# Where the small matrix products of a side chain stand among the wide ones on TensorE (hybrid attention layer, one core)

## What is computed

```python
h = rms_norm(x, pre_w); proj = h @ w_in           # 1024 -> 6152 columns
# branch 1: stick-breaking attention, 8 heads of 64, blocks of 128 keys
z = q @ k.T * 64**-0.5
suffix = cumsum(log_keep, reverse=True) - log_keep # log_keep = -softplus(z), causal
o_sb = (exp(log_sigmoid(z) + suffix) @ v) * silu(gate)
# branch 2: gated delta rule, 4 heads of 128, chunks
q, k, v = silu(causal_conv4(...)); q, k l2-normalised
m = strict(beta * (k @ k.T) * decay)               # unit lower triangular system
u, w = solve(m, [v * beta, k * beta * exp(g)])
for c in chunks:                                   # state S
    v_new = u[c] - w[c] @ S
    o[c]  = (q[c] * exp(g)) @ S + intra[c] @ v_new
    S     = S * exp(g_last) + (k[c] * exp(g_last - g)).T @ v_new
o_gd = rms_norm(o) * silu(gate)
merged = sigmoid(m1) * (o_sb @ w_sb) + sigmoid(m2) * (o_gd @ w_gd)
x = x + rms_norm(merged @ w_out)
```

## Time and profile before

| What | Value |
|---|---|
| median of three runs | 1246.81 us (1245.89 to 1248.23) |
| the profiled execution | 1248.23 us, span 1246.9 us |
| PE busy | 1188.6 us, 95% |
| DVE, ACT, POOL busy | 518.8, 557.8, 471.6 us |
| share of PE in the chain that ended last | 84% |
| wide products L411 | 1536 |

### The profile page before, as it was taken

One profiled execution on the slowest core, in us unless ns is written; L12 is line 12 of the kernel. 1 busy time (PEld: TensorE's weight loads), 2 busy tenths in 40 slices (PEclk: granted clock), 3 DMA queues, 4 the chain that ended last, 5 costly groups with the idle time before them and its releaser, 6 DMA issues.

```text
span 1246.9 us, 15061 instructions
## 1 busy us (share of the span) xinstructions
PE 1188.6 (95%) x5783; PEld 931.0 (75%) x5783; DVE 518.8 (42%) x1092; ACT 557.8 (45%) x1012; POOL 471.6 (38%) x291
## 2 busy tenths in 40 slices
PE   6999999999989999989999999989899999999997
PEld 6777767767657788878677777657888888888886
DVE  4057376575564314153233333332621111644444
ACT  5356466375477653243344444343432222433332
POOL 3344344234343344552222221222444444644441
PEclk9999999999999999989999999978899999999999
DMA  8221120211121233622111111111233333423211
GB/s 240 77 68 52 35 80 23 68 52 34 51 68 35 68 102 102 219 68 56 51 52 51 52 51 51 52 51 51 68 102 93 93 101 101 127 93 102 95 58 68
DMA packets 139801, 95.35 MB, mean 76 GB/s; under 512 B 8801, under 2 KB 124874, under 8 KB 139730
## 3 DMA queue, kind: packets, MB, share of 16 engines
q1 hardware_dynamic: 136112, 89.18, 24.5%
q10 hardware_dynamic: 3618, 5.22, 1.3%
HBM read 91.49 MB, written 2.88 MB: 76 GB/s over the span
## 4 chain that ended last, share of the span: by engine, by line
PE 84%; DVE 8%; ACT 4%; POOL 1%; issue 1%; DMA 0%; ACTq 0%; DVEq 0%
PE bank L411 24%; PE bank L1166 12%; PE bank L1148 12%; PE bank L440 5%; PE bank L808 4%; PE bank L817 3%; PE bank L833 2%; DVE g L1865 2%; PE bank L946 2%; PE bank L631 2%; PE bank L1179 1%; PE bank L958 1%; PE bank L622 1%; DVE g L1862 1%; PE bank L447 1%
## 5 line engine op out<-in xcount | busy, mean ns | idle before, releaser
L2388 POOL TENSOR_TENSOR ring<-raw_ring,ring 128x1024 fp32r<-128x1024 f32 x159 | 386.3, 2433 | 607.0 <-ACT ring L1192 607.0
L411 PE MATMUL bank<-hT,ring 128*128 128x512 f32 x1536 | 406.4, 410 | 4.1 <-POOL ring L2388 3.4
L411 PEld LDWEIGHTS bank<-hT,ring 128*128 128x128 f32 x1536 | 282.7, 192 | 75.0 <-issue 16.4
L1192 ACT CAST ring<-raw_ring 128x1024 fp32r<-128x1024 f32 x160 | 166.7, 1044 | 116.2 <-PE bank L1166 93.8
L1166 PE MATMUL bank<-ring,ring_u 128*128 128x512 f32 x672 | 154.0, 391 | 0.0
L1148 PE MATMUL bank<-hT,ring 128*128 128x512 f32 x672 | 152.5, 389 | 0.0
L1166 PEld LDWEIGHTS bank<-ring,ring_u 128*128 128x128 f32 x672 | 126.2, 188 | 27.6
L1148 PEld LDWEIGHTS bank<-hT,ring 128*128 128x128 f32 x672 | 126.1, 188 | 26.1
L2365 DVE TENSOR_TENSOR ring_u<-u,ring_u 128x1024 fp32r<-128x1024 f32 x32 | 82.4, 2582 | 76.0 <-ACT ring_u L1744 76.0
L2370 DVE TENSOR_TENSOR u<-u 128x512 f32<-128x512 f32 x32 | 22.9, 715 | 139.2 <-ACT u L1751 139.2
L440 PE MATMUL bank<-hT,ring 128*128 128x256 f32 x576 | 70.4, 284 | 2.3 <-DVE hT L1790 2.3
(11 more groups left out here) (297 smaller groups left out, 1615.2 us busy)
## 6 DMA issues: line engine op xcount, KB each, us to landing
raw_ring<-in_w_in SPq DMA_DIRECT2D x144, 256.0 KB, 3.3
raw_ring<-in_w_up SPq DMA_DIRECT2D x64, 256.0 KB, 3.3
raw_ring<-in_w_down SPq DMA_DIRECT2D x64, 256.0 KB, 2.8
raw_ring<-in_w_out SPq DMA_DIRECT2D x32, 256.0 KB, 2.8
x<-in_x SPq DMA_DIRECT2D x4, 512.0 KB, 5.7
raw_ring<-in_w_branch_sb SPq DMA_DIRECT2D x8, 256.0 KB, 2.9
raw_ring<-in_w_branch_gdn SPq DMA_DIRECT2D x8, 256.0 KB, 3.3
x<-in_x ACTq DMA_DIRECT2D x4, 512.0 KB, 6.0
```

The costliest lines, as they stand in the source:

```text
L411: p = pe.matmul(bank, m.slab_k8(n % 4)[:, a, k, :], m.hT[:, b, k, :], start=term == 0, stop=term == 23)
L1192: act.copy(m.ring[:, q, 0, :], m.raw_ring[:, q, :]).then_inc(s.slab_hi[q], 1)
L2388: pool.tensor_tensor(m.ring[:, q, 1, :], m.raw_ring[:, q, :], m.ring[:, q, 0, :].bitcast(F32), ALU.subtract).then_inc(s.slab_lo[q], 1)
```

## The change

Only numbers in `tiles.to` change, and a few calls of it are added or taken out, in the three loop passes and in the merge stage. No instruction is added or removed; DVE, ACT, POOL and the DMA queue keep their lists word for word. On PE the same products stand in another mixture.

```diff
     for i in range(3):
         tiles = Tall(SLABS_A + 8 * (i + 1), 8, tile_a_free(8 * (i + 1)))
-        tiles.to(14)
+        tiles.to(6)
         delta_decay(i)
-        tiles.to(27)
+        tiles.to(16)
         delta_decay_rows(i)
...
-        tiles.to(78)
+        tiles.to(83)
         delta_gram(i)
-        tiles.to(88)
         stick_z(i, 0, 2)
...
-        tiles.to(126)
+        tiles.to(119)
         delta_level_first(i, 4)
+        tiles.to(122)
         stick_log(i, 0, 1)
...
-        tiles.to(140)
+        tiles.to(130)
         stick_log(i, 0, 0)
...
-        tiles.to(146)
+        tiles.to(137)
         delta_solve(i)
-        tiles.to(150)
+        tiles.to(139)
         delta_chunk(i, 0)
+        tiles.to(142)
         delta_from_state(i, 1)
+        tiles.to(144)
         delta_chunk(i, 1)
...
-        tiles.to(165)
+        tiles.to(160)
         delta_o_sum(i)
         tiles.rest()
...
-    tiles.to(64)
+    tiles.to(74)
     delta_k_sum(i)
     delta_v_rows(i)
-    tiles.to(91)
+    tiles.to(94)
     delta_gram(i)
...
-    tiles.to(148)
     delta_level_first(i, 5)
-    tiles.to(164)
+    tiles.to(150)
     stick_log(i, 0, 1)
     stick_log(i, 1, 1)
     delta_level_second(i, 5)
```

More of the change, by code:

```diff
@@ L651, in tensor_program @@
         stick_v_rows(i)
-        tiles.to(60)
+        tiles.to(68)
         stick_z(i, 0, 3)
@@ L656, in tensor_program @@
         delta_v_rows(i)
-        tiles.to(76)
+        tiles.to(81)
         stick_log(i, 0, 3)
         stick_log(i, 1, 3)
-        tiles.to(78)
+        tiles.to(83)
         delta_gram(i)
-        tiles.to(88)
         stick_z(i, 0, 2)
@@ L666, in tensor_program @@
         stick_av(i, 1, 3)
-        tiles.to(102)
+        tiles.to(106)
         stick_log(i, 0, 2)
         stick_log(i, 1, 2)
-        tiles.to(105)
+        tiles.to(112)
         stick_z(i, 0, 1)
@@ L683, in tensor_program @@
         stick_av(i, 1, 1)
-        tiles.to(128)
+        tiles.to(126)
         delta_level_first(i, 5)
-        tiles.to(140)
+        tiles.to(130)
         stick_log(i, 0, 0)
@@ L692, in tensor_program @@
         delta_level_first(i, 6)
-        tiles.to(143)
+        tiles.to(133)
         delta_level_second(i, 6)
-        tiles.to(146)
+        tiles.to(137)
         delta_solve(i)
-        tiles.to(150)
+        tiles.to(139)
         delta_chunk(i, 0)
+        tiles.to(142)
         delta_from_state(i, 1)
+        tiles.to(144)
         delta_chunk(i, 1)
+        tiles.to(147)
+        delta_from_state(i, 2)
+        tiles.to(149)
+        delta_chunk(i, 2)
         tiles.to(152)
-        delta_from_state(i, 2)
+        delta_from_state(i, 3)
         tiles.to(154)
-        delta_chunk(i, 2)
-        tiles.to(157)
-        delta_from_state(i, 3)
-        tiles.to(159)
         delta_chunk(i, 3)
-        tiles.to(165)
+        tiles.to(160)
         delta_o_sum(i)
@@ L722, in tensor_program @@
     delta_decay(i)
-    tiles.to(18)
+    tiles.to(20)
     delta_decay_rows(i)
-    tiles.to(20)
     stick_v_rows(i)
-    tiles.to(56)
+    tiles.to(54)
     delta_q_sum(i)
-    tiles.to(64)
+    tiles.to(74)
     delta_k_sum(i)
     delta_v_rows(i)
-    tiles.to(91)
+    tiles.to(94)
     delta_gram(i)
-    tiles.to(103)
+    tiles.to(106)
     stick_z(i, 0, 3)
     stick_z(i, 1, 3)
-    tiles.to(113)
+    tiles.to(120)
     stick_log(i, 0, 3)
     stick_log(i, 1, 3)
-    tiles.to(114)
+    tiles.to(126)
     stick_z(i, 0, 2)
     stick_z(i, 1, 2)
-    tiles.to(118)
     stick_av(i, 0, 3)
@@ L747, in tensor_program @@
     delta_level_first(i, 4)
+    tiles.to(138)
     stick_log(i, 0, 2)
@@ L750, in tensor_program @@
     delta_level_second(i, 4)
-    tiles.to(137)
+    tiles.to(143)
     stick_z(i, 0, 1)
@@ L761, in tensor_program @@
     delta_level_second(i, 5)
+    tiles.to(155)
     stick_z(i, 0, 0)
@@ L765, in tensor_program @@
     stick_av(i, 1, 1)
-    tiles.to(166)
     delta_level_first(i, 6)
-    tiles.to(176)
+    tiles.to(169)
     stick_log(i, 0, 0)
@@ L771, in tensor_program @@
     delta_level_second(i, 6)
+    tiles.to(175)
     stick_av(i, 0, 0)
     stick_av(i, 1, 0)
-    tiles.to(184)
     delta_solve(i)
-    tiles.to(195)
+    tiles.to(187)
     delta_chunk(i, 0)
-    tiles.to(198)
+    tiles.to(193)
     delta_from_state(i, 1)
-    tiles.to(202)
+    tiles.to(199)
     delta_chunk(i, 1)
-    tiles.to(207)
+    tiles.to(205)
     delta_from_state(i, 2)
-    tiles.to(216)
+    tiles.to(211)
     delta_chunk(i, 2)
-    tiles.to(220)
+    tiles.to(215)
     delta_from_state(i, 3)
@@ L789, in tensor_program @@
     delta_chunk(i, 3)
-    tiles.to(232)
+    tiles.to(230)
     delta_o_sum(i)
```

## The result

| Kernel | Median | Runs |
|---|---|---|
| before | 1247.52 us (1245.89 to 1248.24) | 4 |
| changed | 1259.16 us (1258.36 to 1260.37) | 4 |

The ratio is 1.0104, interval 1.0087 to 1.0121. The forecast was 1254.4 us, within 1249.5 to 1260. So the time is 4.8 us above the one named, and the change is 11.6 us, where 7.6 were forecast. The sign was right, and most of the waits came where they were expected. The likeliest case had a range of its own, 1252 to 1257 us, and that missed. The wide range held narrowly: over all 37 executions of the changed kernel on record the median is 1260.0 us (1257.87 to 1267.25), 12.5 us above the kernel before. Run again beside the kernel before on another chip, the changed one was also 12.5 us slower by the medians, ratio 1.0096 (1.0081 to 1.0111).

A forecast was written before the change was run, and what follows sets the result against it. PE was taken to bound the kernel, so only its waits, clock and returns to wide products could change the time. Passes +4.35, merge stage +3.2 and clock 0 made +7.55 us: 1254.4 us for the median, range 1249.5 to 1260.

The forecast's parts named there:

- The likeliest case: Whole kernel: the forecast itself, a median of 1254.4 us from the summed terms, given 42%.
- end of a pass, L600 to L517: Each pass's end: five more wide products fall into waits and are missing elsewhere, -1.15 us a pass.
- Gram products to level 4, with the port: Each pass: twelve fewer covering products give 1.9 us of new waiting, plus 0.8 for a held port.
- last score block: Each pass, scores to L630: cover falls from 14 to 8 wide products, +0.6 us (0 to +1.0).
- solve to chunk 0: Each pass, before L592: two fewer wide products against a slack of 0.15 us, +0.3 us.
- state chain: Each pass, chunk 0 to chunk 1: wide products between short pairs cover DVE, -1.0 us (-1.2 to -0.5).
- The rival that the chain counts from the last tile: Passes' ends: the five products are not free and L517's wait grows, 3.4 us more, 1257.8 us; 15%.
- The held port: Block 2 in each pass: POOL's SBUF reads block DVE's two L1988, +0.8 us within 0 to +2.6.
- the third rival: Clock: two more 3.4 us stretches at 1.2 GHz, behind the 3 us wait and before level 5, +3.4 us; 12%.
- The clock ... I take 0: Whole kernel: one half-rate stretch may go and one may come, so 0, with 3.4 us to either side.
- Sum of a pass: Loop passes: the terms add up to +1.45 us a pass, counted three times alike, +4.35 us.
- the steps for level 5 and block 0 in the merge stage: Merge stage: 20 fewer products before level 5's second products, +2.0 us; block 0 and `delta_o_sum`, 11 to 9 products, +0.7.

The follow-up runs named there:

- the filled version: Changed kernel with L517's wait in the second and third pass filled by a dummy product and the transposes of `stick_v_rows`: +10.5 us (8.4 to 12.7) against the kernel before.
- the better order: Kernel before, reordered: level 4 onward earlier in passes, state chain spread, `stick_v_rows` before L517, merge stage's block 3 scores later: 1241.28 us against 1247.07, ratio 0.9947.
- The two filled versions of the changed kernel: Changed kernel with L517's wait filled in passes two and three, +10.5 us; the same plus dummies before the merge stage's fourth tile, +12.2; both against the kernel before.
- the experiment: Kernel before with only the merge stage's block 1 logs and level 5's second products after 150 wide products instead of 164: +5.0 us (3.1 to 6.9).

## Why the forecast was right in kind and short in size

| Term | Forecast | Measured |
|---|---|---|
| end of a pass, L600 to L517 | -1.15 | -1.15; third pass -0.7 |
| Gram products to level 4, with the port | +2.7 | +3.04 |
| level 4 to level 5 | 0 | +0.17 |
| last score block | +0.6 | +0.77 |
| solve to chunk 0 | +0.3 | +0.43 |
| state chain | -1.0 | -1.30 |
| **a pass** | **+1.45** | **+1.95; third +2.4** |
| merge: to the Gram products | +1.5 | +0.9 |
| merge: Gram products to level 4 | -0.4 | -0.3, in part by luck |
| merge: level 4 to level 5's second products | +2.0 | +2.2 |
| merge: from there to level 6 | 0 | +0.6 |
| merge: block 0 and `delta_o_sum` | +0.7 | +1.3 |
| merge: the end | -0.6 | -0.3 |
| **merge stage** | **+3.2** | **+4.4** |
| clock | 0 | +1.9 in 4 executions, about +3 in 37 |
| **sum, with 1.9 for the clock** | **+7.55** | **+12.6** |

The measured column is the changed kernel against the one before, beyond the wide products, for the merge stage from the filled version, whose trace has no stretch at 1.2 GHz there. The kernel before has one in the row from the Gram products to level 4, and without it that row would be up to 1.7 us more. The sum of 12.6 stands against 12.5 by the medians on one chip, and against 11.6 and 12.5 by the first four and by all 37 executions; the method itself misses by up to 1.7 us in the table of experiments.

**Right.** The five terms of a pass have the right sign and are within 0.35 us, but for the third pass's end. The rival that the chain counts from the last tile fell, by L1862 and by the eleven free products of the better order. The held port is shown twice. The changed scores bring POOL's split forward just far enough to meet L1988.

**Luck.** The time landed in the band of the third rival, 1258 to 1260 us, to which I had given 12%. That rival is right in part: the clock took 1.9 to about 3 of its 3.4 us. The remaining 3.1 us are waits and small losses that no case had, and the wide range took them in only because it had been stretched for the clock.

**Wrong, the step "The clock ... I take 0".** It is the largest mis-sized term, 0 for 1.9 to about 3 us. I argued that L517's wait would fall to 1.6 us and might spare a stretch. It stayed at 1.9: of the 1.15 us at a pass's end 0.85 came from POOL's wait, and the rest from the restart behind that wait, not from L517. I also set one stretch that might go against one that might come, though the added waits of 2.8 us before the fourth tile were of the length behind which a stretch came nearly each time. In six experiments that added waits the clock took 1.4 to 4.5 us, each uncertain by 1.2 to 2.7. The two filled versions of the changed kernel, which keep most of its waits, show -0.5 and +1.0, so how much a given wait costs in clock stays open.

**Wrong, the step "Sum of a pass".** I counted three like ends. In the third pass only 83 became 86 products, since the merge stage's `delta_q_sum` moved up by two: 0.46 us less. And a small loss at each of the other steps, 0.1 to 0.35 us, all of one sign, makes 2.4 us over three passes, against 0.9 that the state chain gained beyond its term. Nearly all were places where slack was said to be used up and no more.

**Wrong, the steps for level 5 and block 0 in the merge stage.** I priced the first wait of each and took what stands behind for covered. The wait before L566 had the right size, but 0.6 us more is lost behind it up to level 6 (in the experiment as a wait of 0.80 us for ACT), 0.6 us from there to the solve, and L600 waits 0.6 us, since its cover fell from eleven products to nine and the head's last chain had no slack.

## What to carry to other kernels

Ask of each stretch between a step and the one that waits for its outcome whether the other engines or TensorE are longer there, and move fillers only from the second kind into the first: here eleven products at each pass's end were free, and twelve before level 4 cost 1.9 us. When a cover shrinks, price every later step that waits within it, and not only the first. Where TensorE will stand still for two microseconds or more, leave room in the forecast for a lower clock, and compare mean clocks over many executions: four are too few to size it. A stretch at the low clock costs nothing where a wait follows it that it can fall into, so look whether both kernels pay for it.

## What the runs showed of the hardware

- A wait can cost more than its length. The six experiments that added waits to the kernel before had mean granted clocks 0.0011 to 0.0036 below it, and the changed kernel in 37 executions some 0.0025 below its mean over four chips. Kernels that added no wait lay between 0.0005 below and 0.0014 above, and the better order 0.0015 above. The changed kernel with its waits in part filled lay 0.0004 above and 0.0008 below.
- The longer the wait, the more often a stretch of 3.41 us at 1.2 GHz, or two in a row, came with it: 8 of 24 at 1.9 us, 14 of 15 at 2.2 to 3.2 us, 4 of 5 at 2.8 to 3.3 us.
- Such a stretch cost 1.64 us where nothing else waited, and nothing where it fell into a wait for another engine: from the Gram products to level 4 of the merge stage the time beyond the wide products was 10.83 us with it and without.
- In unchanged code the time at 1.2 GHz varied from 49 to 63 us between single executions, and the time of that code from 784.8 to 790.7 us.
- A pair of short products started later behind few wide ones: L592 0.17 us beyond one and 0.09 beyond two; L585 0.25 beyond one, 0.17 to 0.23 beyond two, 0.09 beyond three. Its second step came up to 0.1 us later too.
- A wait that the profile puts down to one engine can have a second one that ends at the same moment, as POOL's split and DVE's L1869 did.
